# Bias of the pool and gate products moved from VectorE into TensorE, and their loads moved to another queue, in a two-block transformer kernel

## The reference

```python
def pool_mixer(x, w_grp, b_grp, scale):          # 4 groups of 256 channels
    ...                                          # windowed means minus x -> pooled
    y = jnp.einsum('bsgc,gcd->bsgd', pooled, w_grp) + b_grp
    return y.reshape(B, S, D_MODEL) * scale

for i in range(DEPTH_2):                         # 2 layers
    mix = pool_mixer(...) if i == 0 else gated_deltanet(...)
    x = layer_norm(DEEPNORM_ALPHA_2 * x + mix, ...)
    ff = squared_relu_mlp(x, mlp_w1[i], mlp_w2[i])
    pe = jax.nn.sigmoid(x @ ple_gate_w[i] + ple_gate_b[i]) * (p[i] @ ple_proj[i])
    x = layer_norm(DEEPNORM_ALPHA_2 * x + ff + pe, ...)
```

## Time and profile before

| | |
|---|---|
| three executions | 2194.54, 2195.71 and 2203.85 us, median 2195.71 |
| the profiled execution | 2203.85 us, span 2202.1 us |
| granted TensorE clock, mean | 0.956 of full |
| busy share | PE 90%, PEld 57%, DVE 42%, ACT 21%, POOL 3% |

### The profile page before, as it was taken

How to read it: one execution, slowest core, us unless ns; L and a number is a source line. 1 busy time by engine, 2 the same in 40 slices (tenths; PEclk the granted TensorE clock), 3 DMA queues, 4 the chain that set the end, 5 groups by cost and what they waited for, 6 DMA issues and landing times. The chain is left out here.

```text
span 2202.1 us, 28567 instructions
## 1 busy us (share of the span) xinstructions
PE 1986.7 (90%) x10949; PEld 1251.8 (57%) x10950; DVE 915.7 (42%) x1459; ACT 457.3 (21%) x525; POOL 60.0 (3%) x121
## 2 busy tenths in 40 slices
PE   4999996999999999999999999779997888869997
PEld 2759774333333333333333343369987888858986
DVE  3489554111111111111111111366646777855654
ACT  2223011010000000000000000125432443324541
POOL 2000002000000000000000000000000000000000
PEclk8999797999999999999999999889998989979999
DMA  9694544959999999899999878455554420134552
GB/s 360 215 322 136 206 173 159 372 209 422 422 422 422 422 422 422 337 422 422 422 422 422 333 320 338 160 186 158 187 194 150 139 72 1 39 127 155 177 189 74
DMA packets 143446, 580.85 MB, mean 264 GB/s; under 512 B 10489, under 2 KB 12521, under 8 KB 94123
## 3 DMA queue, kind: packets, MB, share of 16 engines
q1 hardware_dynamic: 135824, 563.12, 65.9%
q0 software_dynamic: 3040, 11.02, 1.6%
q10 hardware_dynamic: 4507, 5.65, 0.8%
HBM read 578.71 MB, written 1.05 MB: 263 GB/s over the span
## 5 line engine op out<-in xcount | busy, mean ns | idle before, releaser
L1147 PE MATMUL bank<-ring,area 128*64 128x512 f32 x2048 | 461.4, 599 | 28.3 <-DMA ring<-in_w_gu 27.7
L1147 PEld LDWEIGHTS bank<-ring,area 128*64 128x64 f32 x2048 | 144.5, 137 | 327.3 <-issue 236.8
L888 PE MATMUL bank<-area_r,ring_r 128*128 128x256 f32 x992 | 285.3, 288 | 12.9 <-DVE area_r L1997 10.6
L288 DVE TENSOR_TENSOR ring_r<-ring,ring_r 128x2048 fp32r<-128x2048 f32 x92 | 210.8, 2292 | 189.0 <-ACT ring_r L285 188.3
L890 PE MATMUL bank<-area_r,ring_r 128*128 128x256 f32 x992 | 283.3, 286 | 0.0
L891 PE MATMUL bank<-area_r,ring_r 128*128 128x256 f32 x992 | 283.2, 285 | 0.0
L2246 DVE TENSOR_SCALAR area<-bank 128x512 f32<-128x512 f32 x36 | 24.9, 692 | 542.1 <-PE bank L1147 542.1
L285 ACT ACTIVATE ring_r<-ring 128x2048 fp32r<-128x2048 f32 x92 | 175.8, 1912 | 221.1 <-PE bank L891 199.8
L888 PEld LDWEIGHTS bank<-area_r,ring_r 128*128 128x128 f32 x992 | 193.3, 195 | 15.6 <-DVE area_r L1997 10.8
L890 PEld LDWEIGHTS bank<-area_r,ring_r 128*128 128x128 f32 x992 | 193.4, 195 | 0.5 <-issue 0.5
L891 PEld LDWEIGHTS bank<-area_r,ring_r 128*128 128x128 f32 x992 | 193.1, 195 | 0.0
(11 more groups left out here) (329 smaller groups left out, 2076.0 us busy)
## 6 DMA issues: line engine op xcount, KB each, us to landing
ring<-in_w_gu SPq DMA_DIRECT2D x256, 1024.0 KB, 21.1
area<-in_w_dn SPq DMA_DIRECT2D x96, 1024.0 KB, 21.4
ring<-in_mlp_w SPq DMA_DIRECT2D x64, 1024.0 KB, 5.4
ring<-in_w_dn SPq DMA_DIRECT2D x32, 1024.0 KB, 19.9
ring<-in_w_in SPq DMA_DIRECT2D x24, 1024.0 KB, 6.2
ring<-in_gdn_w_in SPq DMA_DIRECT2D x16, 1024.0 KB, 5.5
area<-in_w_mod SPq DMA_DIRECT2D x12, 1024.0 KB, 8.6
ring<-in_w_mod SPq DMA_DIRECT2D x8, 1024.0 KB, 16.6
```

The costliest lines, as they stand in the source:

```text
L288: nc.vector.tensor_tensor(unit_low(i), raw, unit_high(i), ALU.subtract).then_inc(w_split, 1)
L888: ins = mm(out_, a_[0], b_[0], start=start, stop=False)
L1147: ins = mm(bk[hf * BLK:(hf + 1) * BLK, :], x(kt), block_u[:, c:c + BANK], start=False, stop=kt == ND - 1)
```

## The change

Both biases are added by PE, as matmuls of a row of ones with a bias row. The bias rows are loaded to one partition instead of 128. The DVE instructions that added them go away (L2331 two, L2347 eight), with their semaphores; L2327 stays, on one partition, and PE now waits for it too (`scaled` 3). Eight matmuls with 256 columns are added to the pool product, and four with 512 columns to each gate product. `load_ffn` moves from ACT's queue to POOL's, each time behind a wait for the layer norm that comes just ahead of `ffn(i)`, and ahead of POOL's load of the next norm's gain and bias. PE waits for it where it waited before.

```diff
-        pool_scale_bc, pool_b_bc = a(7)[:, 0:D], a(7)[:, D:2 * D]
-        gate_b_bc = area[:, 8 * 2048 + 1024:9 * 2048]
+        pool_scale_bc, pool_b_row = a(7)[:, 0:D], a(7)[0:1, D:2 * D]
@@ POOL
-                 (pool_b_bc, A["pool_b_2"][0].rearrange("(o g) d -> o (g d)", o=1).to_broadcast([P, D])),
+                 (pool_b_row, A["pool_b_2"][0].rearrange("(o g) d -> o (g d)", o=1)),
...
+            def load_ffn(i):
+
+                pool.wait_ge(x_ready, NT * (2 + 2 * i))
+                load((tok(7), A["ple_proj_2"][i].rearrange("(k p) n -> p k n", p=P)),
+                     (area[:, 8 * 2048:8 * 2048 + 512].rearrange("p (t c) -> p t c", t=NT),
+                      A["p_2"][i, 0].rearrange("(t p) c -> p t c", p=P)),
+                     (area[0:1, 8 * 2048 + 1024:9 * 2048], A["ple_gate_b_2"][i:i + 1, :]))
+
+            load_ffn(0)
             load_norm(4)
...
             norm_root()
+            load_ffn(1)
             load_norm(6)
@@ PE
-            pe.wait_ge(scaled, 2)
+            pe.wait_ge(scaled, 3)
...
+                        mm(o, ones[0:1, :], pool_b_row[:, gi * S:(gi + 1) * S], start=True, stop=False)
                         for k in range(2):
                             ins = mm(o, pooled[:, 2 * gi + k, t * P:(t + 1) * P], pw[:, gi, k, :],
-                                     start=k == 0, stop=k == 1)
+                                     start=False, stop=k == 1)
...
-                pe.wait_ge(ffn_in, 48 * (i + 1))
+                pe.wait_ge(late_in, 224 + 48 * i)
...
-                token_major_late(f"gate{i}", f"gate_{i}", x_parts, C)
+                gb = area[0:1, 8 * 2048 + 1024:9 * 2048]
+                token_major_late(f"gate{i}", f"gate_{i}", x_parts, C, bias=gb)
@@ ACT
-            full(act, G("pool_tok", 3))
-            act.wait_ge(alpha_x, 2)
-            load_ffn(0)
...
-                        act.wait_ge(gate_biased, NT * NH * i + NT * s + t + 1)
+                        full(act, g)
...
-            load_ffn(1)
@@ DVE
-            link(v.tensor_tensor(pool_b_bc, pool_b_bc, pool_scale_bc, ALU.mult))
-            for q in range(4):
-                full(dve, G("pooled", q))
-            for t in range(NT):
-                v.scalar_tensor_tensor(x_tok[:, t, :], x_tok[:, t, :], ALPHA2, pool_b_bc, ALU.mult, ALU.add)\
-                    .then_inc(alpha_x, 1)
-            dve.wait_ge(alpha_x, NT)
-            residual("pool_tok", 1.0)
+            v.tensor_tensor(pool_b_row, pool_b_row, pool_scale_bc[0:1, :], ALU.mult).then_inc(scaled, 1)
+            residual("pool_tok", ALPHA2)
...
-                for s in range(NH):
-                    late.below(w0 + 2 * s + 4)
-                    for t in range(NT):
-                        g = G(f"gate_{i}", NT * s + t)
-                        full(dve, g)
-                        v.tensor_tensor(bank(g)[:, :], bank(g)[:, :], gate_b_bc[:, s * BANK:(s + 1) * BANK], ALU.add)\
-                            .then_inc(gate_biased, 1)
+                late.below(w0 + 6)
```

More of the change, by code:

```diff
@@ L469, in build @@
         scaled = sem("scaled")
-        alpha_x = sem("alpha_x")
-        gate_biased = sem("gate_biased")
-        ffn_in = sem("ffn_in")
         windows_ready = sem("windows_ready")
@@ L1683, in _ @@
             experts(act, AC, lambda w: act_block(w, spread_T, y_blk), lambda w: act_block(w, spread_T, y_blk))
[L1685 to L1690, removed]
             late = Splitter(act, "high")
@@ L2340, in ffn @@
                 x_low(f"xT_{i}")
-                dve.wait_ge(ffn_in, 48 * (i + 1))
-                for s in range(NH):
-                    late.below(w0 + 2 * s + 4)
-                    for t in range(NT):
-                        g = G(f"gate_{i}", NT * s + t)
-                        full(dve, g)
-                        v.tensor_tensor(bank(g)[:, :], bank(g)[:, :], gate_b_bc[:, s * BANK:(s + 1) * BANK], ALU.add)\
-                            .then_inc(gate_biased, 1)
+                late.below(w0 + 6)
                 pe_part = tok(6)
```

## The result

| | before | after |
|---|---|---|
| executions timed together | 4 | 4 |
| median (lowest to highest), us | 2198.03 (2194.54 to 2203.85) | 2235.17 (2226.69 to 2237.09) |
| ratio to before, 95% interval | | 1.0141 (1.0107 to 1.0174) |
| profiled execution, span, us | 2202.1 | 2230.0 |

The change makes the kernel 1.4% slower, some 31 us by the ratio, where 12.75 us were forecast. (The ratio takes in all twelve executions of the changed kernel, 2217.68 to 2237.09 us; the medians of the four alone differ by 37 us.) The measured median is 20 us above the upper end of the range.

What follows compares the result with a forecast made beforehand. PE was taken to bound the feed-forward steps, a chain of waits the pool mixer. Pool +1.4, first step +4.1 and second +7.25 us gave +12.75 us on the 2195.71 us median: 2208.5 us, range 2200 to 2215.

Steps and rivals of the forecast that it cites:

- Part 1, PE's work in the pool mixer: Pool mixer: eight added bias matmuls cost PE 1.75 us, 3.5 at half clock; the whole pool mixer +1.4 us.
- Part 1, the rest: Pool mixer: loads land 1.6 us sooner, scaling the bias row adds 1.2 us, removed DVE instructions are worth nothing.
- Part 2: Feed-forward loads on POOL's queue: gate product starts 2.65 us later in the first step, 2.8 us in the second.
- Rival (b): Feed-forward loads land after 5.0 us, 1.95 us less in all, kernel at 2206.6 us; chance 0.13.
- Part 3: Gate products: four bias matmuls with 512 columns on PE cost 2.4 us in each feed-forward step.
- Part 4: Gate products: 4.1 us at half clock cost 2.05 us each; against before, -0.95 us first step, +2.05 us second.
- DVE's relief is worth nothing: Pool mixer and feed-forward steps: taking the bias additions off DVE gains nothing.
- (c): Ring refills share DMA engines with the loads, clock returns late, pool loads gain nothing: 2212.5 us; chance 0.12.

Runs made afterwards that it cites:

- Experiment 3: Changed kernel with pool bias matmuls of 128 rows (bias spread to 128 partitions, scaled by 1/128); ratio 1.0123 to the kernel before.
- 7: Changed kernel with pool bias matmuls of 128 rows, 127 of them zero and only partition 0 loaded; one execution, 2219.68 us.
- 1: Kernel before with only the pool mixer's part of the change; ratio 1.0073 to the kernel before.
- experiment 4: Changed kernel with the eight pool bias matmuls left out, the wait for the scaled row kept; ratio 1.0069 to the kernel before.
- experiment 9: Kernel before with the bias matmuls of the first block's spatial gating given 128 rows, 127 of them zero; ratio 0.9949 to the kernel before.
- Experiment 5: Changed kernel with the feed-forward loads back on ACT's queue at their old, early places; ratio 1.0107 to the kernel before.
- experiment 6: Changed kernel with the gate bias matmuls left out in both layers; ratio 1.0101 to the kernel before.
- experiment 8: Changed kernel with 128-row bias matmuls in pool and gate, and feed-forward loads early on ACT's queue; ratio 1.0060 to the kernel before.

## Why the prediction was wrong

- **Part 1, PE's work in the pool mixer, is the step that failed.** Of the 20 us by which the second block is further from before than forecast, 12.4 are in the pool mixer and the rest in the two feed-forward steps. The part says "eight more matmuls with 256 columns ... 0.22 us each, so 1.75 us", and takes half clock only as twice that. Two things are wrong in it. First the count: a float32 matmul call is two instructions in the profile (the 16 calls are the x32 of the earlier trace rows), so eight calls are 16 instructions, 3.5 us at full clock. The row named the number, and I divided by instructions and multiplied by calls. Second, and larger: I let the bias matmuls cost their own time only. One-row matmuls between full ones kept PE at 1.2 GHz for 21 us while it was busy, so all but the first four of the 24 calls ran at half clock. Experiment 3 shows it (same count and columns, 128 rows, clock back in 3.2 us, 9.3 us less), 7 shows that zeros do as well, and 1, 4 and 9 agree. The product up to the last bank addition took 14.5 us more, not 1.75, and the whole stretch +13.8 us, not +1.4. By an estimate from the rows, some 9 of the 14.5 us are the clock (21.2 us at half clock cost 10.6; the fall in the kernel before had cost 1.7), 3.45 the eight calls at the price of 128-row ones, and some 2 what a one-row call costs beyond that. The kernel before had the same signature at 222.8 us; the prediction took its price of a bias matmul from the same block and didn't read the clock there.
- **Part 1, the rest, held.** The loads were waited for 1.85 us less (1.6 forecast), the scaled row put 1.1 us into PE's way (1.2). The removed DVE instructions were worth nothing: the last bank addition starts 0.11 us behind PE's end in both kernels.
- **Part 2 held.** Landing 6.5 and 6.2 us after the first issue (6.5 and 6.0), gate products 2.6 and 3.0 us later (2.65 and 2.8). PE's idle time ahead of the transposes of `p`, 4.83 and 4.22 us, is above the 3 to 4 that were to be seen. Rival (b), 5.0 us, was too short by 1.5 and 1.2 us. So was the fit in the section "Anatomy of one DMA — SWDGE (gpsimd) path" of the page "DMA: Bandwidth & Descriptors" of the Trainium skill, by which an estimate for this batch is 5.0 us. Experiment 5 shows these waits and the clock that goes with them to be worth 7.5 us in all. The same page of the Trainium skill, section "Rules for kernel authors", says to issue a transfer early and wait for it late. The trace agrees: the 4.83 and 4.22 us of PE's idle time weren't there before.
- **Part 3 was mis-sized by the same count.** The row x2 of the earlier trace rows is one call, not two: 1.05 us for each at full clock, 2.0 at half, 5.2 us in a step instead of 2.4. (The terms as written, "0.9 + 0.5 to 0.9 + 1.04", don't add up to 2.4 either.) In experiment 6 both steps together are 12.5 us shorter without these matmuls, clock included, against 4.8 forecast.
- **Part 4 was mis-sized.** The gate products ran 7.3 and 6.4 us at half clock, counted from their start to the rise, where 4.1 was forecast. For the pause alone the forecast was about right: in experiment 6, with the late loads and no bias matmuls, it was 4.6 and 3.35 us. The other 2.7 and 3.0 us came with the one-row matmuls, and in experiment 5 the clock was lost again just behind one. Its opening words, that PE starts at 0.50 after an idle stretch, don't fit the pool product: in the kernel before it started at 1.00 behind a pause of 2.56 us and fell 0.9 us later. Part 1 had no term for that fall, 1.7 us.
- **"DVE's relief is worth nothing"** held: in experiment 8, with DVE relieved and the two losses removed, the kernel is still 13 us slower (9 to 17).
- The rival on the slower side, (c), was looking at the DMA engines and ended at 2212.5; none of the rivals had the clock falling under a busy PE.

## What to carry to other kernels

Don't move a small addition onto an engine that is the bound, however idle the engine is that it comes from: find the stage's last wait first. If a bias must be a matmul, give it all 128 rows (127 of them may be zero; in experiment 9 that alone took 11 us off), and look at the granted clock of every stretch in which PE is busy, since a busy share of 100% at 0.50 is half a PE. When a price is taken from a trace, check whether the row counts calls or instructions.

## What the runs showed of the hardware that was not expected

- TensorE's granted clock falls from 2.4 to 1.2 GHz with PE busy throughout, where one-row matmuls alternate with full ones: 20.87 busy of 20.90 us at 0.50 in the changed kernel, 18.09 of 18.10 us at 0.51 in the kernel before. With 128 rows, zeros or not, it stays at 1.00 or comes back (after 3.4 us in experiments 3 and 8). PE's busy time in a profile is partly modelled, so short stalls inside it can't be seen; whether the clock answers to the rows themselves or to the extra time that one-row calls take is not shown.
- Beside the clock, one-row float32 calls cost more than full ones. With 128 columns and at full clock a call begins every 0.42 us where every other one has one row, and every 0.22 us where all have 128. In the changed kernel's pool product at full clock, one bias call and two full ones took 1.69 us (1428.81 to 1430.50), where three calls with 128 rows take 3 x 0.44. Why that is stays open.
- In the gate products the longer half clock comes about half from the pause for the loads and half from the one-row matmuls. In the second step it was nothing in the kernel before, 3.35 us with the late loads alone (experiment 6), a fall of 3.4 us with the one-row matmuls alone (experiment 5), and 6.4 us with both. In the first step the kernel before had 6.0 us already, so this step doesn't separate them. Each figure is from one execution.
- Not settled: when the clock falls in the pool product with full matmuls alone. It fell behind a pause of 2.56 us in the kernel before and held behind 1.7 us in experiment 4.
